# Up projection of a gated FFN: block products accumulated in one PSUM bank, partial sums copied out by ScalarE

## The reference

```python
def conv_gated_ffn(x, w_up, conv_w, conv_b, w_down):
    hu = x @ w_up                                  # (1024 x 1024) @ (1024 x 5632)
    s = hu.shape[1]
    hp = jnp.pad(hu, ((0, 0), (CONV_WIDTH - 1, 0), (0, 0)))
    hc = conv_b + conv_w[CONV_WIDTH - 1] * hu      # causal depthwise convolution, width 3
    for i in range(CONV_WIDTH - 1):
        hc = hc + conv_w[i] * hp[:, i:i + s]
    val, gate = jnp.split(hc, 2, axis=-1)          # 2 x 2816
    return (jax.nn.gelu(gate, approximate=True) * val) @ w_down
```

## Time and profile before

| | us |
|---|---|
| median of 3 runs | 2513.73 (2510.49 to 2516.97) |
| the profiled execution, its own time | 2516.51 |
| span of the profile | 2514.7 |
| TensorE busy in the span | 2368.8 (94%) |
| VectorE / ScalarE busy | 1632.9 / 1088.0 |
| the up projection, first to last matmul start | 1854.5 to 2281.6 |

### The profile page before, as it was taken

One profiled execution on the slowest core, in us unless ns is written; L12 is line 12 of the kernel. 1 busy time (PEld: TensorE's weight loads), 2 busy tenths in 40 slices (PEclk: granted clock), 3 DMA queues, 4 the chain that ended last, 5 costly groups with the idle time before them and its releaser, 6 DMA issues. The chain is left out here.

```text
span 2514.7 us, 28722 instructions
## 1 busy us (share of the span) xinstructions
PE 2368.8 (94%) x11156; PEld 1806.4 (72%) x11156; DVE 1632.9 (65%) x1781; ACT 1088.0 (43%) x1290; POOL 397.9 (16%) x276
## 2 busy tenths in 40 slices
PE   7999999949999999986999999998969999998998
PEld 6777566836666666656776778887858888887886
DVE  5552586378999988875212652223589998887877
ACT  4221123237777777765213741112344434333443
POOL 3110100012232222220300210000033232320000
PEclk9999999969999999997999999999989999999999
DMA  5112033379999999976210011114212232216783
GB/s 165 42 42 70 17 119 131 151 264 341 366 382 368 366 362 368 357 265 209 84 51 18 2 50 39 41 50 155 76 34 93 81 96 76 84 59 238 231 292 134
DMA packets 204263, 400.44 MB, mean 159 GB/s; under 512 B 18326, under 2 KB 123798, under 8 KB 187752
## 3 DMA queue, kind: packets, MB, share of 16 engines
q1 hardware_dynamic: 194920, 381.92, 42.8%
q0 software_dynamic: 9216, 16.81, 2.9%
HBM read 360.90 MB, written 47.18 MB: 162 GB/s over the span
## 5 line engine op out<-in xcount | busy, mean ns | idle before, releaser
L143 PE MATMUL up_ps<-blocks_high,up_operand_high 128*128 128x512 f32 x616 | 241.6, 392 | 15.0 <-DVE plain_blocks_rest L3126 11.7
L145 PE MATMUL up_ps<-blocks_high,up_operand_rest 128*128 128x512 f32 x616 | 240.6, 391 | 0.0
L1507 DVE TENSOR_TENSOR expert_rest<-expert_early_raw,expert_high 128x2048 fp32r<-128x2048 f32 x75 | 170.6, 2289 | 23.8 <-ACT expert_high L1501 23.3
L1944 POOL DMA_INDIRECT mixed_residual<-y_rows,row_ids x32 | 105.2, 3288 | 425.8 <-DVE y_rows L1887 425.8
L1501 ACT ACTIVATE expert_high<-expert_early_raw 128x2048 fp32r<-128x2048 f32 x75 | 143.3, 1914 | 27.9 <-DMA expert_early_raw<-in_w_up_dram 11.1
L1507 DVE TENSOR_TENSOR expert_rest<-expert_raw,expert_high 128x2048 fp32r<-128x2048 f32 x60 | 136.4, 2289 | 20.8 <-ACT expert_high L1501 20.4
L143 PEld LDWEIGHTS up_ps<-blocks_high,up_operand_high 128*128 128x128 f32 x616 | 116.4, 189 | 40.7 <-issue 16.8
L3343 DVE TENSOR_TENSOR up_operand_rest<-res,up_operand_high 128x512 fp32r<-128x512 f32 x154 | 143.1, 940 | 3.0 <-ACT up_operand_high L3299 3.0
L1507 DVE TENSOR_TENSOR expert_rest<-res,expert_high 128x2048 fp32r<-128x2048 f32 x57 | 129.7, 2289 | 19.2 <-ACT expert_high L1501 18.8
L144 PE MATMUL up_ps<-plain_blocks_rest,up_operand_high 128*128 128x512 f32 x352 | 137.5, 391 | 0.0
L145 PEld LDWEIGHTS up_ps<-blocks_high,up_operand_rest 128*128 128x128 f32 x616 | 116.5, 189 | 24.5
(11 more groups left out here) (471 smaller groups left out, 6090.5 us busy)
## 6 DMA issues: line engine op xcount, KB each, us to landing
expert_early_raw<-in_w_gate_dram SPq DMA_DIRECT2D x27, 1024.0 KB, 26.0
expert_early_raw<-in_w_up_dram SPq DMA_DIRECT2D x24, 1024.0 KB, 23.0
expert_early_raw<-in_w_down_dram SPq DMA_DIRECT2D x24, 1024.0 KB, 25.3
expert_raw<-in_w_down_dram SPq DMA_DIRECT2D x22, 1024.0 KB, 23.9
res<-in_w_up_dram SPq DMA_DIRECT2D x88, 256.0 KB, 4.0
expert_raw<-in_w_up_dram SPq DMA_DIRECT2D x21, 1024.0 KB, 24.8
res<-in_w_gate_dram SPq DMA_DIRECT2D x20, 1024.0 KB, 25.8
res<-gated_products SPq DMA_DIRECT2D x77, 256.0 KB, 3.2
```

The lines of the kernel that those rows point to most:

```text
L143: nc.tensor.matmul(out, w_high, x_high, start=start, stop=False, skip_group_check=goes_on)
L145: return nc.tensor.matmul(out, w_rest, x_high, start=False, stop=stop, skip_group_check=goes_on)
L1507: self.nc.vector.tensor_tensor(self.rest_part[:, s, :], self.raw[n % RAW_SLOTS], self.high_part[:, s, :].bitcast(F32), ALU.subtract).then_ ...
L1944: pool.indirect_dma_start(m.mixed_dram, bass.IndirectOffsetOnAxis(ap=ids, axis=0), y[:, s, :], None, bounds_check=SEQ - 1, oob_is_err=Fals ...
```

## The change

The order of the jobs of an f becomes P1, P2, P6, P5, P7, P3, P4. The products P1, P6, P7 and P4 are accumulated in one bank (the corner bank, 0 or 1 by the parity of f): only P1 starts a new sum, and the other three go on. So after P6 the bank holds what the join "two" made, after P7 what "three" made, after P4 gate early itself. ScalarE copies the bank out after P1, P6 and P7 (`keep`), and after P4 into `gate_raw`. TensorE may go on in the bank (P6, P7, P4) only when the copy of the state before is done. P2, P5 and P3 have two banks each, by the parity of f. VectorE keeps four joins: P2 into value early, P5 into value late and into gate late, P3 into value late.

On ScalarE, the value's centre tap and the gate's both move to P4 of the same f, and the GELU to P2 of the next f. On VectorE the value taps now come ahead of the gate taps, `gated` comes later by two rests, and the rest ahead of a join moves in places.

```diff
-        NAMES = ("P1", "P2", "P6", "P5", "P7", "P4", "P3")
-        JOINS = ("value_early", "two", "value_part", "three", "gate_late", "gate_early", "value_late")
+        NAMES = ("P1", "P2", "P6", "P5", "P7", "P3", "P4")
+        JOINS = ("value_early", "value_part", "gate_late", "value_late")
+        KEEPS = {"P1": first_part, "P6": two_parts, "P7": three_parts}
...
         def bank(f, name):
-            return ps[:, AT[f, name] % 8, :]
+            first = {"P1": 0, "P6": 0, "P7": 0, "P4": 0, "P2": 2, "P5": 4, "P3": 6}[name]
+            return ps[:, first + f % 2, :]
...
+        def kept(engine, f, name):
+            engine.wait_ge(part_kept, len(KEPT) * f + KEPT.index(name) + 1)
...
         def _(pe):
             for n, (f, name) in enumerate(PLAN):
                 pe.wait_ge(rest_done, n + 1)
-                if n >= 8:
...
+                if name == "P1" and f >= 2:
+                    pe.wait_ge(corner_out, f - 1)
+                if name in READ_BY and f >= 2:
+                    joined_to(pe, f - 2, READ_BY[name])
+                if name in ("P6", "P7", "P4"):
+                    kept(pe, f, {"P6": "P1", "P7": "P6", "P4": "P7"}[name])
+                opens = name in ("P1", "P2", "P5", "P3")
...
-                                   start=(k == 0), stop=(k == H - 1))
+                                   start=(opens and k == 0), stop=(k == H - 1), goes_on=not opens)
...
         def _(act):
+            def gate_centre_of(f):
+                act.wait_ge(used, AT[f, "P4"] + 1)
+                if f:
+                    act.wait_ge(gate_far, f)
+                nc.scalar.activation(gate_raw[:, 0:BANK], bank(f, "P4"), ACT.Copy).then_inc(corner_out, 1)
+                joined_to(act, f, "gate_late")
+                act.wait_ge(corner_out, f + 1)
+                if f:
+                    act.wait_ge(prod, f)
+                centre(f, 1, gate[:], gate_raw, gate_centre)
...
+            def keep(f, name):
+                act.wait_ge(used, AT[f, name] + 1)
+                if f:
+                    joined_to(act, f - 1, {"P1": "value_early", "P6": "value_part", "P7": "gate_late"}[name])
+                nc.scalar.activation(KEEPS[name][:], bank(f, name), ACT.Copy).then_inc(part_kept, 1)
...
             for n, (f, name) in enumerate(PLAN):
                 high(n + AHEAD)
+                if name in KEEPS:
+                    keep(f, name)
+                if name == "P2" and f:
+                    gelu_of(f - 1)
+                if name == "P4":
+                    if f < FT - 1:
+                        value_centre_of(f)
+                    gate_centre_of(f)
...
         def _(dve):
                 rest(f, "P2")
                 if f:
                     dve.wait_ge(value_far, f)
-                dve.wait_ge(first_kept, f + 1)
+                kept(dve, f, "P1")
                 join(f, "P2", value_raw[:, 0:BANK], first_part[:])
+                rest(f, "P6")
+                rest(f, "P5")
                 if f:
                     gated(f - 1)
-                rest(f, "P6")
-                join(f, "P6", two_parts[:], first_part[:])
-                rest(f, "P5")
-                joined_to(dve, f, "two")
+                kept(dve, f, "P6")
                 join(f, "P5", value_raw[:, BANK:SEQ], two_parts[:])
                 rest(f, "P7")
-                join(f, "P7", three_parts[:], two_parts[:])
-                joined_to(dve, f, "three")
+                kept(dve, f, "P7")
                 if f:
                     dve.wait_ge(gate_far, f)
                 join(f, "P5", gate_raw[:, BANK:SEQ], three_parts[:])
+                rest(f, "P3")
                 rest(f, "P4")
-                join(f, "P4", gate_raw[:, 0:BANK], three_parts[:])
-                rest(f, "P3")
-                taps(f, 1, gate[:], gate_raw, gate_centre, gate_near, gate_far)
                 joined_to(dve, f, "value_part")
                 join(f, "P3", value_raw[:, BANK:SEQ], value_raw[:, BANK:SEQ])
                 if f < FT - 1:
                     taps(f, 0, value[:, f % 2, :], value_raw, value_centre, value_near, value_far)
+                taps(f, 1, gate[:], gate_raw, gate_centre, gate_near, gate_far)
```

More of the change, by code:

```diff
@@ L3185, in ffn_up @@
         used = sem("up_operand_used")
-        first_kept = sem("up_first_kept")
+        part_kept = sem("up_part_kept")
+        corner_out = sem("up_corner_out")
         joined = sem("up_joined")
@@ L3195, in ffn_up @@
         taps_at, bias_at = COLS["conv_w_2"][0], COLS["conv_b_2"][0]
-        NAMES = ("P1", "P2", "P6", "P5", "P7", "P4", "P3")
-        JOINS = ("value_early", "two", "value_part", "three", "gate_late", "gate_early", "value_late")
+        NAMES = ("P1", "P2", "P6", "P5", "P7", "P3", "P4")
+        JOINS = ("value_early", "value_part", "gate_late", "value_late")
+        KEEPS = {"P1": first_part, "P6": two_parts, "P7": three_parts}
+        KEPT = tuple(KEEPS)
         PLAN = [(f, name) for f in range(FT) for name in NAMES]
@@ L3215, in bank @@
         def bank(f, name):
-            return ps[:, AT[f, name] % 8, :]
+            first = {"P1": 0, "P6": 0, "P7": 0, "P4": 0, "P2": 2, "P5": 4, "P3": 6}[name]
+            return ps[:, first + f % 2, :]
         def joined_to(engine, f, name):
             engine.wait_ge(joined, len(JOINS) * f + JOINS.index(name) + 1)
-        READ_BY = {"P2": "value_early", "P6": "two", "P5": "gate_late", "P7": "three", "P4": "gate_early", "P3": "value_late"}
+        READ_BY = {"P2": "value_early", "P5": "gate_late", "P3": "value_late"}
+        def kept(engine, f, name):
+            engine.wait_ge(part_kept, len(KEPT) * f + KEPT.index(name) + 1)
         @block.sync
@@ L3305, in centre, with value_centre_of @@
                     .then_inc(centred, 1)
-            def finish(f):
+            def value_centre_of(f):
                 joined_to(act, f, "value_late")
@@ L3312, in finish, with gelu_of @@
                 centre(f, 0, value[:, f % 2, :], value_raw, value_centre)
+            def gate_centre_of(f):
[8 more added lines that the diff above has]
+                centre(f, 1, gate[:], gate_raw, gate_centre)
+            def gelu_of(f):
                 act.wait_ge(gate_far, f + 1)
                 nc.scalar.activation(gate[:], gate[:], ACT.Gelu_apprx_tanh).then_inc(gelu, 1)
+            def keep(f, name):
[3 more added lines that the diff above has]
+                nc.scalar.activation(KEEPS[name][:], bank(f, name), ACT.Copy).then_inc(part_kept, 1)
             for n in range(AHEAD):
```

## The result

Six runs of the changed kernel have a median of 2525.27 us (2520.2 to 2528.87), six of the kernel before 2514.81 (2510.49 to 2516.97). The ratio is 1.0033, 95% interval 1.0022 to 1.0044: 8.3 us slower by the ratio (5.5 to 11.1), 10.5 by the medians. The forecast was 9.4 us.

The account below looks back on a forecast made before the run. The prediction took TensorE, busy 94% of the span, to bound the kernel. Start f = 0 (6.2), f = 1 (1.0), steady state (0) and end (2.2) gave +9.4 us, 2523.1 us on the median, range 2518 to 2530.

Parts of the forecast that it names:

- Removed and added work: Up projection: three VectorE joins fewer per f (45 us over 22 f), three ScalarE copies more; worth nothing by themselves.
- Start, f = 0: First f: TensorE's P6 waits for ScalarE's copy of P1, queued behind its prologue; +6.2 us, bounds 5.4 to 7.0.
- the cold stretch: P6 of f = 0 after its wait: slow matmuls, 4.40 us instead of 2.72, so 1.68 extra.
- Start, f = 1: Second f: TensorE waits for copies of P1 and P6 held by late VectorE and ScalarE; +1.0 us, range 0 to 2.5.
- the forecast wait of 0.3: P6 of f = 1: TensorE waits 0.3 us for the copy of P1, up to 2 if GpSimd slows rests.
- Steady state: Later f: copies wait for TensorE, not the reverse, with some 1.7 us spare in each window; 0 us.
- End: End of the up projection: copy, gate centre and two taps stand exposed behind P4; +2.2 us, bounds 1.9 to 2.5.
- Sum: Whole kernel: 6.2 + 1.0 + 2.2 = +9.4 us, bounds 7.3 to 12.0.
- A: Steady state: copies miss their windows; at 0.5 us for each of 20 f, +10 more, 2533 us; chance 0.10.
- B: Clock: waits cost more cold matmuls, 2526.5 us if two in f = 1, 2558 if every f; chance 0.04.
- C: Start: little more than 5.4 us lost and f = 1 costs nothing, 2520.5 to 2521 us; chance 0.08.
- D: Matmul pace: less PSUM traffic from joins speeds matmuls, 2505 us at 10 ns each; chance 0.06 with others faster.

Follow-up runs that it names:

- e6: Changed kernel with each copy of a partial sum made three times from f = 3 on; stage 439.13 us against 439.04.
- e8: Changed kernel with three VectorE subtractions of 128x512 added in each f, in place of the removed joins; stage 444.58 us.
- e1: Kernel before with only the order changed (P3 ahead of P4, value taps first), seven joins and ring kept; stage 438.08 us.
- e5: Changed kernel with five extra VectorE subtractions (3.5 us in all) behind VectorE's prologue; stage 443.44 us.
- e7: Changed kernel with each copy of a partial sum made five times from f = 3 on; stage 481.28 us.
- e3: Changed kernel with P4 ahead of P3 again, so one bank and four joins without the new order; stage 477.45 us.
- e11: e10 plus the last f's gate centre tap and two taps done in the down projection; stage 434.58 us.
- e9: Kernel before with GpSimd's first weight sums waiting for the first weight rest instead of the first token block's; stage 429.09 us.
- e10: Changed kernel with early copies in f = 0 and f = 1, P3's token block ahead of P4's, first GELU later; stage 435.62 us.

## Why the prediction was right

By its own steps:

- *Removed and added work.* Costed at nothing; for the steady state e6, e8 and the full stretches of TensorE show it. At the start VectorE's time is worth something: given back in e8, it cost 5.5 us. In the stage VectorE's busy time fell from 376.4 to 326.0 us (45 forecast, 50 measured), ScalarE's rose from 177.9 to 217.2 (38 forecast, 39 measured).
- *Start, f = 0.* +6.2 forecast, +7.0 measured. The wait and its releaser were right; the term that was mis-sized is the cold stretch: 1.68 us extra taken over from the one behind the wait of 2.85 us, 2.53 measured behind the one of 11.10. That is the upper edge of the bounds given. In e8 a wait of 10.3 us had eight slow matmuls behind it, here one of 11.1 had twelve. What I didn't see is that P3's earlier place alone would have cost 6.0 (e1), hidden by the copy's wait.
- *Start, f = 1.* +1.0 forecast, 0 measured, with 0.6 us spare. The walk of the other engines was good: from the stage's first matmul, VectorE's last join of f = 0 ends at 35.0 us as forecast, and the copy of P1 at 39.1 (39.2 forecast). But TensorE, held up 0.8 us longer in f = 0, wanted that copy at 39.7 instead of 39.0, and so the forecast wait of 0.3 was gone. The copy of P6 ended at 43.5, 1.4 us earlier than the walk had it, and was wanted at 45.2. e5 and e8 show how thin the first margin was.
- *Steady state.* 0 forecast, 0 measured; spare 1.7 forecast, 1.64 to 1.78 measured (e7). Before, VectorE caught up at 18.2 us an f until about f = 12, and from then on `gated` comes every 19.04 us. In the changed kernel it comes every 19.0 us from f = 3 on, where the walk had the lag gone. The saved time shows there, on an engine that TensorE doesn't wait for.
- *End.* +2.2 forecast, +2.06 measured.
- *Sum.* 9.4 against 9.06 in the stage. Two errors of about a microsecond, at f = 0 and f = 1, offset each other. Part of that is no accident, for what TensorE loses in f = 0 it doesn't wait for in f = 1; that the sum is right to 0.3 us is luck, for 0.7 of the 1.0 in f = 1 was an allowance over the 0.3 that the rows gave.
- *Rivals.* A: excluded by e6 and e7. B: in the changed kernel, behind the stage's first matmuls, no cold stretch but the one at f = 0. None of the short waits in e3 (0.58 to 0.78 us, twice in every f) slowed the matmuls behind it either: behind both rows shown under e3 the matmuls run on at the pace of a full stretch. A start to start of 1.16 and 0.98 us instead of 0.227 costs 0.93 + 0.75 = 1.68 us; the two jobs behind the waits take 2.84 us instead of 2.72, which makes an f of 20.96 instead of 19.04. From f = 1 to the last matmul that comes to 39.5 us, f = 0 took 1.0 more, and the end is 2.1 shorter: 38.4, which is 477.45 - 439.04. Nor did one of the three waits in every f of e7 (0.44 to 0.59 us) bring matmuls at the low clock. So what the Trainium skill says in "TensorE: Matmul & The Clock Gate", in its section on the second failure mode, did not show here, not even with two or three short waits in every f. C and D did not come: the pace stayed at 0.227 us with three copies in place of three joins.

The down projection took 231.14 us from the end of the stage to the end of the span, against 230.24. In the experiments it lies between 229.9 and 232.2 without order, so I put no cause to this 0.9.

## What to carry to other kernels

A ring of buffers hides lateness, and the trace shows how much: compare when a result is ready with when its reader comes. Before replacing such a ring by one accumulator with copies in between, look at that distance at the start of the stage, not at the busy shares; work taken off an engine that holds nobody up bought nothing in the steady state here, while the slack that went with it was paid at the first job. And find out which edit makes which part of the loss: here two causes stood in the same place, and removing one only brought out the next.

## What was not expected of the hardware

- The matmuls behind a long wait ran at 0.43 us apiece instead of 0.227, at a granted clock of 0.50 instead of 1.00: seven of them behind 2.85 us of waiting in the kernel before, twelve behind 11.1 in the changed one, but eight behind 10.3 in e8. What sets their number between seven and twelve stays open.
- Waits of 2.44, 2.52 and 2.8 us (e11, e5, e8) had some seven slow matmuls behind them, and between the wait and the first slow one stood a few, one in e8 and five in e5, at full pace. A wait of 2.03 us in e9 had eight, the one of 1.63 us in e10 and those of up to 0.93 in all kernels had none. The f with such a wait of 2.4 to 2.8 us took 4.3 to 4.6 us longer than 19.04.
- A VectorE subtraction of 128x512 with a GpSimd sum beside it took 1.75 us instead of 0.68, and the sum up to 3.3 instead of 1.3. In e9, where the sums were brought forward, the rests paid.
